# A flat loop of visits for the expert stage, quarter-form steps for experts of at most 32 tokens, and the first step ahead of the second gather half

## The reference

```python
logits = h @ w_router                    # 256 tokens x 8 experts
top_val, top_idx = lax.top_k(logits, 2)  # two experts for each token
gate = jax.nn.softmax(top_val)
# for each expert e, over the tokens that chose it:
ys = (silu(xb @ w_gate[e]) * (xb @ w_up[e])) @ w_down[e]   # 1024 -> 3584 -> 1024
out[token] += gate * ys
```

## Time and profile before

| what | value |
|---|---|
| median of 3 runs | 1670.78 us (1669.82 to 1673.24) |
| the profiled execution's own time | 1672.14 us |
| its span, first to last instruction | 1670.4 us |
| mean granted TensorE clock | 0.969 |
| TensorE busy | 1544.0 us (92%) |
| VectorE / ScalarE busy | 418.1 us (25%) / 250.2 us (15%) |
| read from HBM | 482.63 MB, 290 GB/s over the span |

### The profile page before, as it was taken

How to read it: one execution, slowest core, us unless ns; L and a number is a source line. 1 busy time by engine, 2 the same in 40 slices (tenths; PEclk the granted TensorE clock), 3 DMA queues, 4 the chain that set the end, 5 groups by cost and what they waited for, 6 DMA issues and landing times.

```text
span 1670.4 us, 21757 instructions
## 1 busy us (share of the span) xinstructions
PE 1544.0 (92%) x8696; PEld 852.4 (51%) x8697; DVE 418.1 (25%) x955; ACT 250.2 (15%) x560; POOL 0.2 (0%) x4
## 2 busy tenths in 40 slices
PE   5988889999989998599999999999999999999996
PEld 2777658777657774444444443443333443333332
DVE  2366525333344533600002000110000300003003
ACT  2132210000012331110101010011111111111112
POOL 0000000000000000000000000000000000000000
PEclk8999799999999998799999999999999999999998
DMA  9974525765656440068979797999999999997991
GB/s 348 380 266 164 189 101 192 273 252 202 227 193 229 172 178 16 1 264 332 407 289 407 284 408 294 408 374 405 408 407 407 407 377 407 407 408 296 367 377 78
DMA packets 168185, 484.43 MB, mean 290 GB/s; under 512 B 10024, under 2 KB 20544, under 8 KB 168000
## 3 DMA queue, kind: packets, MB, share of 16 engines
q1 hardware_dynamic: 168128, 483.70, 75.8%
HBM read 482.63 MB, written 1.05 MB: 290 GB/s over the span
## 4 chain that ended last, share of the span: by engine, by line
PE 79%; DMA 9%; DVE 5%; SPq 3%; ACT 2%; issue 2%; DVEq 0%; ACTq 0%
PE bank L1024 11%; PE bank L931 9%; PE bank L1064 8%; DMA ring<-in_w_exp_up 8%; PE bank L778 7%; PE bank L1008 6%; PE bank L1185 6%; PE bank L1020 5%; PE bank L949 4%; PE bank L912 4%; PE bank L1058 3%; PE bank L1211 3%; PE bank L772 3%; SPq L629 2%; PE bank L1280 2%
## 5 line engine op out<-in xcount | busy, mean ns | idle before, releaser
L1024 PE MATMUL bank<-ring,hT 128*64 128x448 f32 x1280 | 255.1, 546 | 32.2 <-DMA ring<-in_w_exp_up 12.7
L1024 PEld LDWEIGHTS bank<-ring,hT 128*64 128x64 f32 x1280 | 89.0, 137 | 190.7 <-issue 153.7
L931 PE MATMUL bank<-hT,ring 128*128 128x256 f32 x704 | 158.0, 385 | 1.7 <-DVE hT L1429 1.7
L778 PE MATMUL bank<-hT,ring 128*128 128x256 f32 x640 | 153.0, 396 | 3.9 <-ACT hT L1953 2.5
L1809 DVE TENSOR_TENSOR bt<-arena,bank 64x512 f32<-64x512 f32 (+2 forms) x36 | 24.3, 675 | 493.5 <-PE bank L1024 249.6
L931 PEld LDWEIGHTS bank<-hT,ring 128*128 128x128 f32 x704 | 135.2, 193 | 24.1 <-issue 3.8
L778 PEld LDWEIGHTS bank<-hT,ring 128*128 128x128 f32 x640 | 124.5, 198 | 26.0 <-DVE hT L1429 4.4
L1064 PE MATMUL bank<-ring,bt 128*32 128x256 f32 (+1 forms) x1232 | 136.8, 445 | 0.0
L1348 DVE SCALAR_TENSOR_TENSOR acc<-ring,cond,acc 128x512 f32<-128x512 f32 x140 | 105.2, 752 | 4.9
L1020 PE MATMUL bank<-ring,hT 128*128 128x448 f32 x256 | 100.7, 546 | 4.1 <-DMA ring<-in_w_exp_up 3.4
L1008 PE MATMUL bank<-ring,hT 128*32 128x448 f32 x1024 | 102.8, 542 | 0.0
(11 more groups left out here) (279 smaller groups left out, 1179.8 us busy)
## 6 DMA issues: line engine op xcount, KB each, us to landing
ring<-in_w_exp_gate SPq DMA_DIRECT2D x128, 896.0 KB, 9.2
ring<-in_w_exp_up SPq DMA_DIRECT2D x128, 896.0 KB, 13.0
ring<-in_w_exp_down SPq DMA_DIRECT2D x64, 1536.0 KB, 15.9
ring<-in_w_ada SPq DMA_DIRECT2D x24, 2048.0 KB, 9.4
ring<-in_w_in SPq DMA_DIRECT2D x10, 2048.0 KB, 12.8
ring<-in_w_exp_down SPq DMA_DIRECT2D x32, 512.0 KB, 16.3
ring<-in_w_ff_gate SPq DMA_DIRECT2D x5, 2048.0 KB, 12.4
ring<-in_w_ff_up SPq DMA_DIRECT2D x5, 2048.0 KB, 12.8
```

The costliest lines, as they stand in the source:

```text
L778: last = mm(o[:, 0:T], w[:, k, t * P:(t + 1) * P], hT[:, k, :], start=(k == 0), stop=(k == KC - 1))
L931: last = mm(bank[n % 2][:, a * T:(a + 1) * T], w[a][:, k, t * P:(t + 1) * P], hT[:, k, :], start=(k == 0), stop=(k == KC - 1))
L1024: last = mm(o[64 * c2:64 * c2 + 64, 64 * c2:64 * c2 + EH], xsT[:, k, t0:t0 + 64], w[:, k, c2 * EH:(c2 + 1) * EH], start=(k == 0), stop=(k ...
```

## The change

- The nested loops become one loop over 21 visits (`VISITS`). A table of 106 numbers gives for each visit its first job, the number of ends so far, whether it has a small step, which large expert it has (0 for none) and which end follows (0 to 3). Each engine with a part in it (TensorE, VectorE, ScalarE) loads these five values at the head of each visit, and the class of the large or small expert where there is one. Every step's body stands once in the code.
- The visits are: the first small step alone, with end 3; a large one alone; small; small and large; small with end 1; small and large; small; small and large; small with end 2 (that is place 1 with 0 and 2); four of small and large at places 4 and 3; four at places 6 and 5; four large steps alone. The order of the 32 steps is as before.
- A new class 0 holds experts of at most 32 tokens. Its step (`tiny_step`) takes gate and up in quarters, waits for a gate and an up piece at a time, and goes down in quarters. Three of the four small experts (25, 28 and 10 tokens) have this class. The places are dealt so that the 54-token expert is at place 4 and 28, 10 at places 2 and 6.
- The second gather half, the large window, the clearing of `ys` and of banks 4 to 6 and the start of `yacc` move from before the first step into end 3, that is behind the first small step. The second half now fills banks 4, 5, 6 and 1.
- End 1 scatters both tiles instead of one.

```diff
-STREAM_AT = (0, 1, 3, 5, 7, 2, 4, 6)
+STREAM_AT = (0, 1, 3, 5, 7, 4, 6, 2)
...
+TINY = 32
+UNITS = {0: [("quarter", 0)], 1: [("half", 0)], ...
...
+        def planned(eng, at, u, most):
+            return eng.value_load(plan_i[0:1, bass.ds(u + at, 1)], min_val=0, max_val=most)
...
-            for h in range(2):
+            def gather(h, banks):
                 pe.wait_ge(sel_v, 2 + h)
...
+            gather(0, range(4))
...
+            def tiny_step(J, ends):
+                pe.wait_ge(xsS_v, ends + 1)
+                pe.wait_ge(yacc_v, 4 * ends + 12)
+                for k in range(0, KC, 2):
+                    pe.wait_ge(full_g[k // 2], 16 * J + 16)
+                    pe.wait_ge(full_u[k // 2], 16 * J + 16)
+                    quarter(TX, range(k, k + 2), True)
+                pe.wait_ge(yzS_v, ends + 1)
+                pe.wait_ge(eh_v, 4 * J + 4)
+                h, one_ = hs[64:P, 0, :], ident[64:P, 64:P]
+                mm(bank[3][:, 0:64], h[:, 0:P], one_, start=True, stop=True)
+                for t in range(1, 4):
+                    last = nc.tensor.transpose(bank[3][:, t * 64:(t + 1) * 64], h[:, t * P:(t + 1) * P], one_)
+                last.then_inc(et_p, 4)
+                down(J, 0, 0, ALL, (0,), 7)
...
-                pe.wait_ge(xsS_v, 1)
-                turn_scatter_weights(0, bank[3])
-                with nc.Fori(0, 4, engines=PE, head_slot={PE[0]: 0}) as l:
...
+                with nc.Fori(0, NV, engines=PE, head_slot={PE[0]: 0}) as u:
+                    J, ends, has, large, end = (f(pe, u) for f in (job_at, ends_seen, has_small, large_no, end_of))
+                    with pe.If(has != 0):
+                        tiny = class_at(pe, 2 * ends)
+                        with pe.If(tiny == 0):
+                            tiny_step(J, ends)
+                        with pe.Else():
                             small_step(J, ends)
+                    with pe.If(large != 0):
+                        which = large_class(pe, large)
                         with pe.If(which == 3):
+                            large_step(large, J + has, ends, 3)
                         with pe.Else():
+                            large_step(large, J + has, ends, 2)
+                    with pe.If(end != 0):
+                        with pe.If(end == 3):
+                            gather(1, SECOND_BANKS)
+                            turn_scatter_weights(0, bank[0])
+                            pe.wait_ge(sgt_a, 1)
+                        with pe.Else():
+                            stream_scatter(ends, (0, 1))
...
             with ve.If(misfit == 0):
-                stream_weights(0)
                 gathered(0)
                 small_window(None)
-                gathered(1)
-                large_window(1)
...
+                nc.vector.memset(bank[7][:, 0:T], 0.0).then_inc(yacc_v, 4 * NE + 1 - 20)
+                nc.vector.memset(bank[7][:, T:], 0.0).then_inc(yzS_v, 1)
+                with ve.Fori(0, NV) as u:
...
+                        with ve.If(end == 3):
+                            stream_weights(0)
+                            gathered(1)
+                            large_window(1)
+                            signal(nc.vector.memset(ys, 0.0), dv)
+                            then(nc.vector.tensor_copy(yacc, xs[:, :, :]))
+                            for i in (4, 5, 6):
+                                last = nc.vector.memset(bank[i][:, :], 0.0)
+                            last.then_inc(yzL_v, 1)
+                            ve.wait_ge(sgt_p, 1)
+                            stream_weights(1)
...
+                with ae.If(class_at(ae, 2 * g) == 0):
+                    for c in (0, 1):
+                        ins = act(ys[64:96, 1, c * T:(c + 1) * T], bank[7][32 * c:32 * c + 32, 0:T], ACT.Copy)
+                    ins.then_inc(ys_a, 1)
+                with ae.Else():
+                    act(ys[64:P, 1, 0:CW], bank[7][0:64, :], ACT.Copy).then_inc(ys_a, 1)
...
+                        with ae.If(end == 3):
+                            gathered(1, SECOND_BANKS)
+                            scatter_weights_in(0, bank[0])
```

More of the change, by code:

```diff
@@ L72 @@
 C_PLAN = C_IOTA + NE
-NPLAN = 40
-C_END = C_PLAN + NPLAN
 ADA = 6 * D // CW
@@ L247 @@
             JOBS.append((small_, 2 * s_ % ES + 1))
-AHEAD_OF_LARGE = [n - 1 for n, (pos_, _) in enumerate(JOBS) if pos_ % 2]
-ENDS_SEEN = [0, 0, 1, 1] + [2] * 4 + [3] * 4 + [4] * 4
 JOBS_DONE = [12, 20, 28, 32]
+VISITS = []
+small_left, ends_, j_ = ES, 0, 0
+while j_ < len(JOBS):
+    has_, large_ = JOBS[j_][0] % 2 == 0, 0
+    visit_ = [j_, ends_, int(has_), 0, 0]
+    j_ += has_
+    small_left -= has_
+    end_ = 3 if has_ and j_ == 1 else int(has_ and ends_ == 0 and small_left == 0)
+    end_ = 2 if has_ and j_ in JOBS_DONE else end_
+    if not end_ and j_ < len(JOBS) and JOBS[j_][0] % 2:
+        visit_[3] = JOBS[j_][0] // 2 + 1
+        j_ += 1
+    if not end_ and (j_ == len(JOBS) or j_ in JOBS_DONE):
+        end_ = 2
+    visit_[4] = end_
+    ends_ += end_ in (1, 2)
+    VISITS.append(visit_)
+NV = len(VISITS)
+PLAN = [v[0] for v in VISITS] + [len(JOBS)] + [v[k] for k in range(1, 5) for v in VISITS]
+NPLAN = len(PLAN)
+C_END = C_PLAN + NPLAN
 TX = 3 * P // 2
+SECOND_BANKS = (4, 5, 6, 1)
 SPLIT = 2 * P
@@ L271 @@
 CAPS = (64, 96, 160)
-UNITS = {1: [("half", 0)], 2: [("half", 0), ("quarter", 64)], 3: [("wide", 0), ("quarter", 128)],
+TINY = 32
+UNITS = {0: [("quarter", 0)], 1: [("half", 0)], 2: [("half", 0), ("quarter", 64)], 3: [("wide", 0), ("quarter", 128)],
          4: [("wide", 0), ("wide", 128)]}
@@ L1011, in quarter @@
                             last.then_inc(u_used if q == 3 else g_used, 1)
+                        elif alone and k == KC - 2 and q % 2:
+                            last.then_inc(eu_p if q == 3 else eg_p, 3)
             def stream_hidden(J, n, i, a, t0, c=0):
@@ L1806, in stream_step @@
                     up_ready(J, n, i)
-                    rows_, o = (slice(64, P), bank[2]) if n > 1 and i == ITEMS[n] - 1 else (slice(0, P), bank[1])
+                    rows_, o = (slice(64, P), bank[2]) if n != 1 and i == ITEMS[n] - 1 else (slice(0, P), bank[1])
                     n_ = EH if n == 3 and i < 2 else CW
@@ L1831, in stream_end @@
                         large_out(2, jobs)
-                nc.vector.tensor_copy(ys[64:P, 1, CW:D], bank[7][64:P, :]).then_inc(ys_v, 1)
+                with ve.If(class_at(ve, 2 * g) == 0):
+                    for c in (2, 3):
+                        last = nc.vector.tensor_copy(ys[64:96, 1, c * T:(c + 1) * T], bank[7][32 * c:32 * c + 32, 0:T])
+                    last.then_inc(ys_v, 1)
+                with ve.Else():
+                    nc.vector.tensor_copy(ys[64:P, 1, CW:D], bank[7][64:P, :]).then_inc(ys_v, 1)
                 small_window(2 * g + 2)
@@ L1869, in _ @@
-                last.then_inc(yzL_v, 1)
-                ve.wait_ge(sgt_a, 1)
-                nc.vector.memset(bank[7][:, :], 0.0).then_inc(yzS_v, 1)
-                with ve.Fori(0, 4) as l:
-                    which = class_at(ve, 2 * l + 1)
-                    with ve.Fori(0, ES) as i:
-                        J = job_ahead(ve, l, i)
-                        with ve.If(l != LONE):
+                nc.vector.memset(bank[7][:, 0:T], 0.0).then_inc(yacc_v, 4 * NE + 1 - 20)
+                nc.vector.memset(bank[7][:, T:], 0.0).then_inc(yzS_v, 1)
@@ L1877, in _ @@
+                with ve.Fori(0, NV) as u:
+                    J, ends, has, large, end = (f(ve, u) for f in (job_at, ends_seen, has_small, large_no, end_of))
+                    with ve.If(has != 0):
+                        with ve.If(class_at(ve, 2 * ends) == 0):
+                            stream_step(J, 0)
+                        with ve.Else():
                             stream_step(J, 1)
-                        with ve.If(which == 3):
-                            stream_step(J + 1, 3)
+                    with ve.If(large != 0):
+                        with ve.If(large_class(ve, large) == 3):
+                            stream_step(J + has, 3)
@@ L1880, in _ @@
                         with ve.Else():
-                            stream_step(J + 1, 2)
-                        with ve.If(l == 0):
-                            stream_step(J + 2, 1)
-                            with ve.If(i == 1):
-                                stream_end(0)
-                    stream_end(l + 1, which)
+                            stream_step(J + has, 2)
+                    with ve.If(end != 0):
+                        with ve.If(end == 3):
[9 more added lines that the diff above has]
+                            stream_weights(1)
+                        with ve.Else():
+                            jobs = job_at(ve, u + 1)
+                            with ve.If(end == 1):
+                                stream_end(0, jobs)
+                            with ve.Else():
+                                stream_end(ends, jobs, large_class(ve, ends))
```

(2 more changed lines are left out.)

95 lines of the change are left out of this document (44 added, 51 removed).

## The result

The changed kernel takes 1707.8 us (median of 4 runs, 1707.4 to 1708.6), the kernel before 1670.6: a ratio of 1.022, 95% interval 1.0203 to 1.0238. Slower, as forecast, but by 37.2 us where 10.9 were forecast, and outside the range. The profiled span is 1706.2 us against 1670.4, the mean granted clock 0.931 against 0.969.

A forecast was written before the change was run, and what follows sets the result against it. Loads bound most of the stage, TensorE the lone steps and part of place 1. Terms 8.8 - 1.3 - 6.1 + 8.9 + 0.6 = +10.9 on 1672.14 gave 1683.0, less 1.36: 1681.6 us; 8-in-10 range 1667 to 1692.

The forecast's parts named there:

- part 2: Place 1, quarter form: periods stay load-bound, only the excess of the first two goes; -1.3 us, between -2 and 0.
- part 4: Lone steps: four more serial register loads and branches at each of three borders; +8.9 us, between +6 and +10.
- part 1: Start: earlier first step, but fetch stalls and register loads delay the first large step; +8.8 us, between -3 and +16.
- The second stall that I took: Start: entering the new class-3 body stalls TensorE's sequencer between 3.6 and 6.0 us, taken as 4.8.
- more stalls: Rival: each body's first entry costs up to 6 us, in the start or at places 3 and 4; about 1690 us; 0.12.
- Part 3: After the ends: tiny steps bring back load time lost behind two ends; -6.1 us, between -7 and +3.
- the rival for place 1: Clock falls in tiny steps; large steps two to four lose 1.7 us each: +5.1, 1686.7 us; chance 0.08.
- Part 5: Last two ends: class load, branch and two copies for one, 0.3 us each; +0.6 us (0 to 2).
- No stall: Rival: no fetch stall, loads as priced; start -0.5, sum +1.6, 1672.4 us, no change; chance 0.18.
- head start survives: Rival: loads and fetches pass under the array's work at start and lone borders; -9.8, 1661.0 us; chance 0.14.

The follow-up runs named there:

- the filler: Changed kernel with eight unused 512-column products behind each lone step, as work for the array while the sequencer loads: 1718.6 us, ratio 1.028.
- the four kernels with one word and loads between the lone steps: Changed kernel with five visit values in one word: 1688.1 us; also gather between steps: 1674.1; or gather ahead of loop: 1673.8; first combination with class-2 body first: 1671.4.
- the two unpacked kernels with a repaired start: Changed kernel, still five loads per visit, with second gather half between small and large step: 1691.5 us; or ahead of the loop as before: 1692.6 us.

## Why the prediction was right in direction and wrong in size

The forecast was +10.9 us, and +37.2 were measured. Two steps of it failed most: that place 1 stays at the pace of the loads whatever TensorE's sequencer does (part 2), and that a gap between lone steps costs only its own length, with nothing put down for the clock (part 4). The start (part 1) had its stalls in the wrong places. Step by step:

**Part 1, start: +8.8, measured +13.4.** The first step began within 3 us of the forecast, just as much earlier as the gather was. Its products took the 7.9 us forecast at the lower clock. Its down part took 5.56 and not 3.5: +2.1. The clock came back during the products (1.00 from 698 to 702 us), as I had it, but in the serial piece TensorE stood for 2.8 us and more, and the down part ran at 0.56. Ahead of the gather I took one first jump; there were two in a row, over the small and over both large bodies (3.7 + 7.4 us), and a gap of 9.45 us where 5.0 was forecast: +4.4. The gather itself, also at the lower clock, took 8.85 us for 8.0. The second stall that I took, 4.8 us for the class-3 body, was not there, since that body is reached in sequence: the large step follows the gather's end after 7.8 us, not 11.3. The error is in *where* the stalls are. I had put two bodies jumped over in a row down as one stall, and a second stall on entering a new body; the long branches are all jumps. The earlier trace rows had shown just that, a jump over the class-2 body. The Trainium skill ("Runtime: NRT & Kernel Launch", section "Instruction fetch mechanics") has sequential code prefetched and a taken branch out of the window stall; the trace agrees, with 3.7 to 7.4 us for four such jumps, a block of the queue "instruction" in each, and nothing for the class-3 body. It does not bear out that every long jump is such a one: later jumps over the same bodies took 0.2 us. In the prediction I had quoted this and then charged the sequence.

**Part 2, place 1: -1.3, measured +13.7. This is the step that failed most.** I had the first period as bound by the loads, and put down no more stall in it than the 3.17 us of before. In the flat loop the way from the first large step to the next small one goes over the class-2 body and then over the block of the ends, each for the first time (6.0 + 5.7 us), and then through five loads. My own rival "more stalls" had something near it, but as a cost of entering a body, in the start or at places 3 and 4, and gave it 0.12. The second mistake is in the slack: I set TensorE's 75 us against 77.9 us of loading as if any order would do. But SBUF holds one step only, and the next loads wait for the small step's own releases. So a small step that starts 11 us late holds the queue back, to 0 GB/s from 803 to 807. The runs take the period apart one by one: 105.5 us as changed, 100.3 with the gather moved (the stall at the block of the ends is gone), 97.8 with the loads packed as well, and 92.9 with the class-2 body put first besides. My term of -1.3 was also not the 2.0 us that the two excesses of the earlier trace rows add up to; without the stalls the gain may be there, as the last of these periods is at the loads' pace.

**Part 3, after the ends: -6.1, measured -6.6. Right,** and for its reason: 3.2 and 3.4 us at the two ends where 3.0 and 3.1 were forecast, and at the second the kernel without the quarter form gives the 3.4 back.

**Part 4, lone steps: +8.9, measured +15.1.** The gaps are as forecast (3.7 us, +3.0 each, 8.9 in all). The step that failed is the clock: I had charged 1.7 us for it in the start, by the earlier trace rows, and in the rival for place 1, but not here, where TensorE was busy up to the gap. Four loads added to the kernel before show both, and the filler shows the clock's share alone: 1.6, 3.0 and 1.8 us at the three borders. The same thing gave +2.5 at place 3, where the forecast had nothing: gaps of 3.5 us, and behind them 7.9 us for 32 records that took 6.2 before.

**Part 5, the ends: +0.6, measured +0.6** (0.2 and 0.4 in the table). Differences this small are within the noise of one execution.

**The rivals.** "No stall" and "head start survives" both fell: the gaps at the lone borders were near 4 us, and branches over 3 us stood in the trace. The clock did fall in tiny steps of place 1 (the down part takes 5.5 us at 908 and 3.3 at 1096), but that did little there: the third period is 92.9 us for 92.6. Where it cost was the first step, which is on the path. Clock and stalls, which I had weighed as alternatives at 0.08 and 0.12, came together and in other places. A range whose upper end adds only one of them was too short.

**What stays open.** Why a gap of 1.5 to 1.9 us cost the clock at three of the twelve borders in the four kernels with one word and loads between the lone steps. Why the period with end 1 is 86 us in the two unpacked kernels with a repaired start, when it is 82 in the changed kernel. Whether the first jumps take longer for a larger body or for busier DMA queues: they were 3.7 us over the smallest and 7.4 over the largest, but 3.6 at the end of the stage. And what decides whether a first jump stalls at all: those over the quarter form's body (0.33 us, small experts all in class 1) and over the scatter (0.29 and 0.23) did not, and the block of the ends did although half of it had run.

## What to carry to other kernels

Count for each engine the jumps that it takes over code it has not run, in the order of the first pass: the long ones cost 3.7 to 7.4 us here, and the transfers of the queue "instruction" show until when they are to be looked for. Put bodies in the order of their first use, and see that the first visit runs through as much of the code as it can. Control values between two steps that TensorE bounds are dearer than their own time, since a gap of 3.5 us also took the clock for the next 3 to 6 us: pack them in a word, or give a run of equal steps a loop without loads. Where the weights of one step fill the buffer, slack is not the period less the busy time, but how late each step may release its pieces.

## What the runs showed of the hardware

- In the changed kernel the first jumps over the class-1 body, both large bodies, the class-2 body and the block of the ends stopped TensorE's sequencer for 3.7 to 7.4 us, and a block of the queue "instruction" passed within each; later ones of the same lines took 0.2 us. Three first jumps over other code not yet run took 0.23 to 0.33 us. The class-3 body, reached in sequence, showed no stall.
- Gaps of 3.5 to 4.0 us between lone steps were followed each time by slower first products (15 borders of 15 in five kernels), at 1.6 to 3.0 us each; the granted clock, read at two of them, was 0.61 and 0.50. Behind gaps of 0.66 to 0.74 us in the kernel before, and behind six of six gaps of 1.5 us, they were at full speed; behind gaps of 1.8 and 1.9 us they were slower in three of six.
- 16 records of a product with 128x128 weights and 512 columns took 7.06 us, 0.44 each.
